# A weight item's low part subtracted on POOL in two instructions, one per 128-row chunk

## What is computed

```python
def second_block(x, ...):
    for l in range(DEPTH):
        h = x @ w_cols
        ...
        mix = jnp.concatenate([o_gla, o_rwkv, o_nsa], axis=-1) @ w_out[l]
        x = _layer_norm(DEEPNORM_ALPHA * x + mix, ln1_w[l], ln1_b[l])
        ffn = (jax.nn.silu(x @ ffn_w_gate[l]) * (x @ ffn_w_up[l])) @ ffn_w_down[l]
        x = _layer_norm(DEEPNORM_ALPHA * x + ffn, ln2_w[l], ln2_b[l])
```

## Time and profile before

| what | value |
|---|---|
| median of 3 runs | 1650.04 us (1649.4 to 1652.15) |
| the profiled execution, its own time | 1656.09 us |
| its span | 1654.3 us |
| busy PE / DVE / ACT / POOL | 1545.1 / 731.2 / 786.2 / 970.6 us |
| mean granted clock of PE | 0.966 |
| POOL: L179 | x412, 970.4 us |
| ACT: L172 | x412, 415.5 us |

### The profile page before, as it was taken

The page is one execution under the profiler, slowest core; times in us unless marked ns, Lnnn a source line. Parts: engine busy times, 40 slices in busy tenths (PEclk is TensorE's granted clock), DMA queues, the critical chain, the costliest instruction groups (busy, mean ns, idle before and its releaser), DMA issues. The chain is left out here.

```text
span 1654.3 us, 20605 instructions
## 1 busy us (share of the span) xinstructions
PE 1545.1 (93%) x7896; PEld 1270.5 (77%) x7896; DVE 731.2 (44%) x1078; ACT 786.2 (48%) x1230; POOL 970.6 (59%) x416
## 2 busy tenths in 40 slices
PE   8999899999998989897988889999889989899998
PEld 6887787888877878676787768888767778677886
DVE  3224854551248545328455651110456555831102
ACT  5545575445446644465443434443464443444442
POOL 6887358888873578575000468878652000578786
PEclk9999999999999999999999799999999888999999
DMA  7665335656653365563301247656543201356564
GB/s 229 181 178 154 89 103 165 190 167 176 179 162 85 107 203 166 150 175 104 103 1 51 78 127 217 183 169 194 153 120 101 71 1 52 107 152 187 158 186 139
DMA packets 121632, 227.96 MB, mean 138 GB/s; under 512 B 10304, under 2 KB 26176, under 8 KB 121536
## 3 DMA queue, kind: packets, MB, share of 16 engines
q1 hardware_dynamic: 120384, 222.46, 45.4%
q10 hardware_dynamic: 1152, 4.19, 0.8%
HBM read 225.58 MB, written 1.05 MB: 137 GB/s over the span
## 5 line engine op out<-in xcount | busy, mean ns | idle before, releaser
L179 POOL TENSOR_TENSOR parts<-raw,parts 128x1024 fp32r<-128x1024 f32 (+5 forms) x412 | 970.4, 2368 | 669.9 <-ACT parts L172 667.4
L210 PE MATMUL ps<-parts,xT 128*128 128x512 f32 (+4 forms) x2624 | 820.2, 390 | 19.5 <-issue 4.5
L172 ACT CAST parts<-raw 128x1024 fp32r<-128x1024 f32 (+5 forms) x412 | 415.5, 1013 | 442.5 <-PE ps L210 244.0
L210 PEld LDWEIGHTS ps<-parts,xT 128*128 128x128 f32 x2624 | 493.8, 191 | 127.9 <-issue 12.9
L210 PE MATMUL ps<-parts,x_low 128*128 128x512 f32 (+3 forms) x672 | 255.1, 388 | 0.0
L210 PE MATMUL ps<-parts,M_low 128*128 128x512 f32 (+2 forms) x640 | 245.0, 387 | 0.0
L210 PEld LDWEIGHTS ps<-parts,x_low 128*128 128x128 f32 x672 | 129.3, 193 | 24.4 <-issue 1.2
L210 PEld LDWEIGHTS ps<-parts,M_low 128*128 128x128 f32 x640 | 121.0, 189 | 20.5
L210 PE MATMUL ps<-parts,aT 128*128 128x512 f32 x352 | 109.5, 395 | 0.0
L210 PE MATMUL ps<-parts,H_low 128*128 128x512 f32 x272 | 105.9, 394 | 0.0
L210 PEld LDWEIGHTS ps<-parts,aT 128*128 128x128 f32 x352 | 66.0, 188 | 15.6
(11 more groups left out here) (338 smaller groups left out, 1905.9 us busy)
## 6 DMA issues: line engine op xcount, KB each, us to landing
raw<-in_w_in SPq DMA_DIRECT2D x160, 512.0 KB, 3.6
raw<-in_ffn_w_down SPq DMA_DIRECT2D x44, 512.0 KB, 4.4
raw<-in_ffn_w_gate SPq DMA_DIRECT2D x40, 512.0 KB, 3.8
raw<-in_ffn_w_up SPq DMA_DIRECT2D x40, 512.0 KB, 3.8
raw<-in_w_out SPq DMA_DIRECT2D x32, 512.0 KB, 3.6
raw<-in_w_branch SPq DMA_DIRECT2D x24, 512.0 KB, 3.4
raw<-in_w_mem_kv SPq DMA_DIRECT2D x16, 512.0 KB, 3.4
raw<-in_w_in SPq DMA_DIRECT2D x16, 366.0 KB, 3.3
```

Source lines behind the costliest of these rows:

```text
L172: self.nc.scalar.copy(self.part(i, 0)[:, 0:nk, 0:w], self.raw(i)[:, 0:nk, 0:w]).then_inc(self.hi_ready.sem, 1)
L179: self.nc.gpsimd.tensor_tensor(self.part(i, 1)[:, 0:nk, 0:w], self.raw(i)[:, 0:nk, 0:w], self.part(i, 0)[:, 0:nk, 0:w], ALU.subtract).then ...
L210: ins = pe.matmul(b[:, 0:w], a(k0 + 2 * n + c, t), self.part(i, lo_w)[:, c, 0:w], start=(opens and n == p == 0), stop=(final and p == len( ...
```

## The change

For an item of two chunks POOL issues two subtractions, one for each chunk of 128 rows, with no wait between them. Only the second raises `lo_ready`, so all waits on that semaphore have the values of before.

```diff
         for k, i in enumerate(self.split_items):
             _, nk, w, _ = self.items[i]
             pool.wait_ge(self.hi_ready.sem, k + 1)
-            self.nc.gpsimd.tensor_tensor(self.part(i, 1)[:, 0:nk, 0:w], self.raw(i)[:, 0:nk, 0:w],
-                                         self.part(i, 0)[:, 0:nk, 0:w], ALU.subtract).then_inc(self.lo_ready.sem, 1)
+            for c in range(nk):
+                ins = self.nc.gpsimd.tensor_tensor(self.part(i, 1)[:, c, 0:w], self.raw(i)[:, c, 0:w],
+                                                   self.part(i, 0)[:, c, 0:w], ALU.subtract)
+            ins.then_inc(self.lo_ready.sem, 1)
```

## The result

The changed kernel takes 1660.31 us in the median of 6 runs (1657.18 to 1670.08), against 1650.78 for the kernel before in 6 runs beside them. The ratio is 1.007, with a 95% interval of 1.0042 to 1.0099: slower by 0.7%, a small difference but clear of the noise, where 1639 and a gain had been forecast. The profiled execution took 1670.08 us, 10 above its median; a second profile, of the same program in experiment e1_again, took 1660.2 where that experiment's median was 1664.99. What follows is read in both.

What follows compares the result with a forecast made beforehand. PE, busy for 93% of the span, was taken as the bound, not POOL's own time. Gains of 5.2 + 3.2 + 4.5 + 1.0 = 13.9 us, less 3, gave 11: median from 1650.0 to 1639, range 1630 to 1652.

Steps and rivals of the forecast that it cites:

- First block: 0: First block: DVE's holds lie where PE hardly idles behind DVE, or in runs of two-input operations; gain 0.
- the end of the mixer: Mixer's end, both layers: x is ready earlier, so PE starts its transposes earlier; 2.6 us gained, twice: 5.2.
- some 0.5: Mixer's end: part of PE's earlier start, some 0.5 us, lost again to the last item of the next step.
- the gain is taken back: Rival, 0.18: holds fall, but PE stands at later items; mixer's end gives 1 for 5, keys 1 for 4.5; 1646.
- The rotated keys: Rotated keys: DVE finishes them earlier, so PE waits less; 3.0 us in layer 1, 1.5 in layer 0, together 4.5.
- The RWKV preparation: Preparation of the RWKV terms: shorter holds cut PE's wait by 2.6 us, 0.6 in layer 1; together 3.2.
- The norm behind the first feed-forward net: Norm after the first feed-forward net: the second L2044, held to 3.321 us, is held less; 1.0 us gained.
- the hand-over between halves: Between an item's two POOL instructions: DVE gets the port, so a held operation loses 0.8 to 1.1 us, not 2.1.
- the rival to which 0.13 was given: Rival, 0.13: POOL retakes the port between halves, so DVE is held for both; 4.5 us slower, 1654.5.
- 0.15 us an item: POOL, all 412 items: the second instruction adds 0.15 us each, 62 us in all, covered by PE.
- the supply becomes the bound: Rival, 0.06: long DMA landings plus 0.15 us per item make PE wait in the feed-forward nets; 13 us, 1652.
- the text gave 3 as its sign: Sign: DVE faster, but PE's waits on POOL and ACT's casts up by over 3 us: supply has taken the gain.

Runs made afterwards that it cites:

- e1_again: The changed kernel as it is, run and profiled a second time; 1.0078 of the kernel before, 1664.99 us.
- e3: Against the kernel before: items halved in the first block only, whole in the second; 1.0051, 1658.94 us.
- e9: Against the kernel before: only ten items halved, those in the first block's two gapless stretches (67 to 71, 167 to 171); 1.0024, 1657.74 us.
- e5: The changed kernel, all items halved, with ACT's conversion of xT moved ahead of the cast of gate item 4; 1.005 of the kernel before.
- e10: The changed kernel with 34 items whole, in the first block's gapless stretches and at both mixers' ends; 1653.65 us against 1653.33 for the kernel before, 1.0011.
- the copy of the kernel before: The kernel before, unchanged, run again for a second profile; ratio 1.0007, profiled span 1651.7 us.
- e11: Against the kernel before: only five items halved, 218 to 222, at the RWKV preparation of layer 0 in the second block; 1.0017.
- after: The first profiled execution of the changed kernel, set matmul by matmul beside the kernel before; span 1668.3 us against 1654.3.
- e4: Against the kernel before: items whole in the first block, halved in the second; 1.0065, 1660.71 us.
- e2: The changed kernel's two instructions per item, but cut at column 4 of both chunks, so one piece is tiny; 1.0083 of the kernel before.

## Why the prediction was wrong

**The step that failed is the price of DVE's turns on POOL's side.** It was left out in "First block: 0" and taken as covered at the end of the mixer. The first block first. The prediction looked only for what DVE's shorter holds bring there, found that PE has no idle time behind DVE, and entered nothing. It did not ask what DVE's doubled turns cost POOL where items follow without a gap. The price was in the same text, 0.46 us for a 512-column operation let in, and was applied at the mixer only. e3 and e9 measured it: steps of 2.0 and 4.6 us for the block, of which ten items make 2.1 and 3.0, though in layer 1 some of it is won back right behind. The Trainium skill, SBUF — State Buffer, on the shared port pair, has the lock "held for the full instruction"; the traces agree, since the hold of L957 shrank with the instruction, from 2.815 to 1.701 us. The cost is on the other side: where DVE has an operation waiting, it gets in after each half, and an item of POOL then carries up to two turns (2.87 us before, 3.98 after, item 68).

**The end of the mixer, 5.2 gained in the forecast, 2.8 and 2.3 lost.** This is the largest miss of the sum, 10.3 us. DVE's part was right: x needed 3.33 us, not 6.34, and PE's wait for it fell by 7.9 us. The forecast took "some 0.5" as lost again to the last item. e5 shows that all of it is lost, and to the supply: with the conversion ahead of the cast, PE waits on POOL. e10, with the items there whole, has neither loss. This is the rival "the gain is taken back" and more: the text had the fourth item late by 1.0 us and took that to be covered, where the next step's gate items come late too, and so the sign turns.

**The rotated keys, 4.5 forecast, 0 measured.** The 3.0 for layer 1 was read from a wait of 3.65 us which the copy of the kernel before does not have; PE's waits for H at these transposes are 5.3 us in all after the change, as before (3.65 + 1.66), and the longer one is 3.2 where the copy's was 2.74. The wait of 1.66 in layer 0, which the copy does have, became 2.1 in place of shorter by 1.5. For layer 1, what one execution happened to show was entered as a gain of the program.

**The RWKV preparation, 3.2 forecast, 1.6 measured,** in layer 0; in layer 1 nothing. The wait of L1293 went from 6.4 to 4.4 us, as said. In the same kernels the quiet stretch behind it costs 4.2 to 5.0 us more (2.5 in e11), at the lower clock. No term of the sum was about the clock, which over the whole kernel makes 7 to 8 us of the loss by the estimate above, and what sets it off stays open.

**The norm behind the first feed-forward net, 1.0 forecast, 0.2 measured.** PE's two waits for x there were 4.0 us in all and are 3.8: the hold of 3.321 us did shrink, but PE gained next to nothing by it.

**Right were:** the hand-over between halves, against the rival to which 0.13 was given; POOL at 1030 to 1060 us (1040.3); the holds (1.701, 2.235 us); DVE's busy time down by 60 us (62.1, though 50.5 against the copy, whose own 719.6 shows how far one kernel's executions differ here); and that 0.15 us an item is covered in the places that e10 splits. The rival *the supply becomes the bound* was right in kind, since PE's waits on POOL and on ACT's work behind the casts grew by 19.7 us where the text gave 3 as its sign. Its sum is slightly off as well: at a landing of 4.8 us it comes to 0.08 us an item and 11 us, not 0.09 and 13. Its cause was another: it had the ring's landing time plus 0.15 us an item as the trigger, in the feed-forward nets, and what came late were items drawn out by DVE's turns, in the first block and at the mixer.

Together, from the table for after: 6.6 in the first block, 5.1 at the mixers, 4.2 in the quiet stretch, less 1.6 at the preparation and less 1.0 that PE regains between 600 and 640 us, make 13.3 us of the 14.0 by which that profile is longer. That it comes so near is partly luck: the 2.3 ahead of 232 us and others left out cancel, and in e1_again the same places make 10.7 us while its span grew by 4.2. The medians give 9.5 and, in e1_again, 14.3. That the split of the items in the first block's gapless stretches and at the mixers causes most of the loss is shown by e10, which leaves these 34 whole and can't be told from the kernel before; its mean granted clock is 0.9642 against 0.9658, so a part of the clock's loss went with them; e3 and e9 show the waits of the first block, e4 those of the mixers. How much of each step is waiting and how much is the clock is not parted but for layer 1 (e9), the 4.2 is only placed, and e2's loss is not explained by these places.

## What to carry to other kernels

When two engines wait for each other as DVE and POOL do here, shortening one engine's instructions does not only shorten the other's waits: the other engine gets more turns, and its work is put in front of yours. Price both directions at every place where the split engine works without a gap, above all where prefetched items are the only slack and other work is queued behind the casts that wait for them. Take a wait that carries a term of the sum from two profiles, not one. And compare the engine's idle time and its granted clock before you read its waits: here the idle time was the same, and the matmuls were slower.

## What the runs showed of the hardware

- A POOL subtraction of 8 elements per partition takes 0.205 us in the median (0.273 in the mean, e2), and DVE is let in behind it as behind a long one. From start to end, two pieces of 512 take 2.548 us in the median, 0.144 more than one of 1024 (2.404); 8 and 1016 take 2.554.
- Two executions of one program can differ by 10 us in one stretch (1267 to 1412 us: -0.2 in after, -10.4 in e1_again), with the same instructions in the same order.
- Items halved near 750 us go with an interval of 10.2 us at 1.2 GHz between 827 and 844 us, where POOL does nothing. A wait of 2.25 us at 597 us went with a granted clock of 0.89 in that window in the kernel after, and an equal one of 2.26 us in e9 with none of it (1.00). So a wait of this length goes with either.
